# Latent attention scores by three passes over high and low parts, with the heads in two slots

## The chip, the cores and the metric

One core of one Trainium2 chip runs the whole program. The metric is the device time of one execution in microseconds (us); lower is better. All inputs and outputs are float32.

## What is computed

Two transformer blocks, one after the other, over 1024 tokens of width 1024. The change lies in the second block's latent attention (4 heads; each query and key has 128 plain and 64 rotated components; the rotated key is shared by the heads). Cut to what matters:

```python
q = (_rmsnorm(c_q, q_a_norm_w) @ w_uq).reshape(b, s, 4, 192)        # 128 plain + 64 rotated
kv = (_rmsnorm(c_kv, kv_a_norm_w) @ w_ukv).reshape(b, s, 4, 256)    # 128 key + 128 value
q_m = _rmsnorm(concatenate([q_nope, rope(q_rope)]), mla_q_norm_w)   # over 192
k_m = _rmsnorm(concatenate([k_nope, rope(k_rope)]), mla_k_norm_w)
s = einsum('bqhd,bkhd->bhqk', q_m, k_m) * 192 ** -0.5               # all 1024 keys, no mask
o = einsum('bhqk,bkhd->bqhd', softmax(s), v)
x = x + concatenate([o_mla, o_diff]) @ w_out
```

The second block also has a differential attention (ahead of the latent one) and an MLP (behind it). Nothing of the first block, of the differential attention or of the MLPs is changed.

## The kernel before

Activations lie transposed in SBUF: features in the 128 partitions, the 1024 tokens along the free dimension.
The order of the work is one list `S` of stages, written out by hand; each engine walks through all of `S` and issues its own part of each stage, so an engine that waits for one stage is not at the next. PSUM has two `big` tiles (128x1024), handed out by `take`, which waits until the reader of the tile's last use is done, two `tbank` tiles for transposes and two `obank` tiles for the outputs.

The latent part of `S`: the products `cq0`, `cq1`, `ckv`, `krope`, their norms, `uqr` (rotated queries of two heads at a time into `mqr[0]`, `mqr[1]`), then for each head h: `mh` h (24 matmuls at line 829: query, key, value, each drained by VectorE at line 1479), `v_t` (8 transposes of the values at line 870, copied out by ScalarE at line 1173), and for q and k each: `mn0` (ScalarE squares, line 1433; VectorE adds the rotated squares, line 1846), `mn1` (sum over the partitions by a product with ones, line 858), `mn2` (ScalarE takes the inverse root, Ln and Exp, lines 1185 and 1187; VectorE scales the plain and the rotated rows, lines 1853 and 1857). Heads 0 and 1 have `mh` and `v_t` ahead of the loop, heads 2 and 3 inside it.

The loop is `attend_pairs` over 32 units (4 heads x 4 steps x 2 query tiles of 128). In each iteration TensorE issues `sc` of the next unit (scores: 128 queries by 1024 keys, line 987; for each half of the keys one matmul over the 128 plain rows and one over the 64 rotated rows), then what `early` names, then half of the pair of the step before: `pv` part 0 (transposes of the probabilities, line 1010, and two of four groups of line 1028) or part 1 (the other two groups), then what `late` names. VectorE drains each score tile with its minimum (line 1705), later scales the probabilities (`nm`, lines 1725 and 1727); ScalarE takes the exponential (line 1221) and copies transposed probabilities out of PSUM (line 1173). `mn1` and `mn2` of the next head stand in iterations u + 2 and u + 4 of a head (u = 8h), ahead of `pv` part 0. `y2split` splits outputs for the next product and stands in the last head's odd iterations.

The queries and keys of all four heads have buffers of their own (`mqn`, `mkn`, `mqr`, `mkr`).

Of the kernel before, what the change touches and what calls it, by code (L numbers as in the profile page):

```python
# [15 lines left out]
F32 = mybir.dt.float32  # L16
# [97 lines left out]
def _emit(nc, ctx, known, a):  # L114
# [90 lines left out]
    sqr = [at(f"sqr{s}", G1 + 4 * K + 4 * K * s, [P, T]) for s in range(3)]  # L205
    cqf = [at(f"cqf{s}", G1 + 16 * K + 4 * K * s, [P, T]) for s in range(3)]
    krb = at("kr_b", G1 + 28 * K, [P, T])
    clh = at("cl_hi", G1 + 32 * K, [P, 3, T], F32R)
    cll = at("cl_lo", G1 + 44 * K, [P, 3, T], F32R)
    mqn = [at(f"mqn{h}", G2 + 4 * K * h, [P, T]) for h in range(4)]  # L210
    mkn = [at(f"mkn{h}", G2 + 16 * K + 4 * K * h, [P, T]) for h in range(4)]
    mqr = [at(f"mqr{p}", G2 + 32 * K + 4 * K * p, [P, T]) for p in range(2)]
    mkr = [at(f"mkr{p}", G2 + 40 * K + 4 * K * p, [P, T]) for p in range(2)]
    mvb = [at(f"mv{h}", G2 + 48 * K + 4 * K * h, [P, QT, P]) for h in range(4)]
    mpt = [at(f"mpt{s}", o, [P, HALF]) for s, o in enumerate((G2, G2 + 2 * K, G2 + 16 * K))]
    sqn = [at(f"sqn{s}", G1 + 16 * K + 4 * K * s, [P, T]) for s in range(2)]
    mrt = at("mrt", G1 + 24 * K, [P, T])
    mvf = at("mv_f", X0 + 28 * K, [P, T])
    sskv = at("ss_kv", G1 + 60 * K, [P, T])
    krz = at("kr_z", G1 + 56 * K, [P, T])  # L220
# [52 lines left out]
    s_hn = sig("head_normed")  # L273
    s_ptu = sig("pt_used")
# [310 lines left out]
    add("mh", 0)  # L585
    add("v_t", "mv0")
    for q in "qk":
        add("mn0", q, 0)
# [3 lines left out]
    add("mh", 1)  # L592
    add("v_t", "mv1")
    early, late = {}, {}
    for h in range(4):
        u = 8 * h
        if h == 3:
            late[u + 1] = [("y2split", 4), ("y2split", 5)]
            late[u + 3] = [("y2split", 6), ("y2split", 7)]
            late[u + 5] = [("y2split", 0), ("y2split", 1), ("y2split", 2)]  # L600
        else:
# [1577 lines left out]
```

## Time and profile before

| | |
|---|---|
| median of 3 runs | 3427.17 us (3426.89 to 3434.18) |
| the profiled execution | 3439.09 us |
| its span, first to last instruction | 3437.2 us |
| mean granted TensorE clock | 0.962 |
| TensorE matmul busy | 3188.8 us, 93% of the span |
| VectorE / ScalarE / GpSimd busy | 1214.4 / 1047.4 / 990.8 us |

How to read it: the span is the profiled execution less 1.9 us around it. Busy times of the engines overlap each other. "PEld" is the loading of TensorE's stationary operand, which can run beside a matmul. The end of a matmul is modelled, so the distance between starts is what to read for its cost. The granted clock is 1.0 at 2.4 GHz and 0.5 at 1.2 GHz.

### The profile page before, as it was taken

Reading aid. Unit: us, or ns where it says so; the run is one execution under the profiler, and the core shown is the slowest. Engines: PE = TensorE matmul, PEld = TensorE weight load, DVE = VectorE, ACT = ScalarE, POOL = GpSimd, SP = SyncE. Lnnn points to the kernel's source line nnn. Section 1 sums busy time; section 2 is a strip of 40 time slices with the busy share of each in tenths; the row PEclk is TensorE's granted clock in tenths of the full one; section 3 lists DMA queues with packets and bytes.
Section 4 is the critical chain, followed back from the end, with each engine's and each line's share of the span. In section 5 each row is a group of like instructions: output and inputs, shape, how many; then the busy total and the mean of one; then the engine's idle time right before and its main releaser. Section 6 shows DMA issues by size and latency. Waiting matters only on the chain. (4 is left out here: it accounts for less than half of the span.)

```text
span 3437.2 us, 36710 instructions
## 1 busy us (share of the span) xinstructions
PE 3188.8 (93%) x14286; PEld 2369.7 (69%) x14286; DVE 1214.4 (35%) x2184; ACT 1047.4 (30%) x1472; POOL 990.8 (29%) x416
## 2 busy tenths in 40 slices
PE   5989888888989999999999889887999999999998
PEld 3556555565778788888887556564446788888887
DVE  4347777766132111111113555734333211111111
ACT  3235544444442211111124344533333211111110
POOL 4322324121234343343347100031001332324241
PEclk8879998999999999999999999998999999999999
DMA  5311112111252111111111301010002111111112
GB/s 158 100 25 36 39 31 50 38 49 38 62 183 62 44 48 55 43 49 49 49 43 37 109 24 30 7 45 14 7 0 74 43 55 43 54 44 49 49 49 67
DMA packets 261614, 176.22 MB, mean 51 GB/s; under 512 B 20661, under 2 KB 248885, under 8 KB 260917
## 3 DMA queue, kind: packets, MB, share of 16 engines
q1 hardware_dynamic: 261496, 174.64, 17.5%
q8 instruction: 75, 1.23, 0.2%
q14 instruction: 43, 0.34, 0.0%
HBM read 142.60 MB, written 25.20 MB: 49 GB/s over the span
## 5 line engine op out<-in xcount | busy, mean ns | idle before, releaser
L829 PE MATMUL big<-g_hi,w_hi 128*128 128x512 f32 x3328 | 1072.8, 404 | 59.2 <-ACT gst_b L1247 21.1
L829 PE MATMUL big<-g_lo,w_hi 128*128 128x512 f32 x3328 | 1041.4, 394 | 0.0
L829 PE MATMUL big<-g_hi,w_lo 128*128 128x512 f32 x3328 | 1038.1, 393 | 0.0
L829 PEld LDWEIGHTS big<-g_hi,w_hi 128*128 128x128 f32 x3328 | 611.1, 191 | 257.1 <-issue 131.3
L829 PEld LDWEIGHTS big<-g_lo,w_hi 128*128 128x128 f32 x3328 | 633.2, 190 | 137.3 <-issue 0.7
L829 PEld LDWEIGHTS big<-g_hi,w_lo 128*128 128x128 f32 x3328 | 631.8, 190 | 137.5 <-issue 0.4
L1875 POOL TENSOR_TENSOR w_lo<-w_raw,w_hi 128x1024 fp32r<-128x1024 f32 x99 | 241.6, 2440 | 765.8 <-ACT w_hi L1149 765.8
L1953 POOL TENSOR_TENSOR w_lo<-w_raw,w_hi 128x1024 fp32r<-128x1024 f32 x76 | 181.9, 2394 | 64.2 <-ACT w_hi L1367 64.2
L1818 DVE TENSOR_TENSOR x_res<-big,x_res 128x1024 f32 x40 | 49.0, 1225 | 382.1 <-PE big L829 382.1
L1979 POOL TENSOR_TENSOR w_lo<-w_raw,w_hi 128x1024 fp32r<-128x1024 f32 x40 | 95.7, 2392 | 273.2 <-ACT w_hi L1395 273.2
L1173 ACT ACTIVATE pt<-tbank 128x512 f32<-128x512 f32 (+1 forms) x160 | 88.0, 554 | 221.8 <-PE tbank L1010 221.8
L1395 ACT ACTIVATE w_hi<-w_raw 128x1024 fp32r<-128x1024 f32 x40 | 42.4, 1060 | 327.4 <-PE big L829 327.4
L1964 POOL TENSOR_TENSOR g_lo<-t_act,g_hi 128x1024 f32 x32 | 76.7, 2397 | 217.1 <-ACT g_hi L1376 217.1
L1797 DVE TENSOR_TENSOR t_g<-big,r_rep 128x1024 f32<-128x1024 f32 x32 | 39.2, 1225 | 274.0 <-PE big L829 274.0
L1643 DVE TENSOR_SCALAR_CACHE_REDUCE tally_a<-idx_acc,edge 128x384 f32<-128x384 f32 (+2 forms) x147 | 126.6, 861 | 5.2
L1149 ACT ACTIVATE w_hi<-w_raw 128x1024 fp32r<-128x1024 f32 x99 | 103.7, 1047 | 74.0 <-PE big L829 57.0
L1376 ACT ACTIVATE g_hi<-t_act 128x1024 f32 x32 | 34.0, 1061 | 298.6 <-DVE t_act L1801 298.6
L1010 PE MATMUL tbank<-ident_sb,prob 128*128 128x128 f32 x576 | 97.5, 291 | 23.2 <-ACT prob L1215 21.0
L1915 POOL TENSOR_TENSOR gst_b<-gst_b,r_rep 128x1024 f32<-128x1024 f32 x16 | 38.3, 2391 | 273.6 <-ACT gst_b L1247 273.6
L1215 ACT ACTIVATE prob<-prob,rc 128x256 f32<-128x256 f32 (+7 forms) x128 | 92.1, 767 | 78.7 <-DVE rc L1718 78.7
L1010 PEld LDWEIGHTS tbank<-ident_sb,prob 128*128 128x128 f32 x576 | 71.5, 148 | 53.0 <-issue 19.2
L1790 DVE TENSOR_TENSOR t_act<-big,t_silu 128x1024 f32<-128x1024 f32 x22 | 26.9, 1225 | 214.3 <-PE big L829 214.3
(253 smaller groups left out, 3423.9 us busy)
## 6 DMA issues: line engine op xcount, KB each, us to landing
w_raw<-in_w_up SPq DMA_DIRECT2D x54, 512.0 KB, 4.0
w_raw<-in_w_in SPq DMA_DIRECT2D x51, 512.0 KB, 4.1
w_raw<-in_w_down SPq DMA_DIRECT2D x48, 512.0 KB, 4.1
w_raw<-in_w_gate SPq DMA_DIRECT2D x22, 512.0 KB, 3.8
rot<-rope_in SPq DMA_DIRECT2D x68, 128.0 KB, 2.3
g_spill<-gst_b SPq DMA_DIRECT2D x16, 512.0 KB, 3.0
x_res<-x_spill SPq DMA_DIRECT2D x2, 4096.0 KB, 14.6
w_raw<-in_w_out SPq DMA_DIRECT2D x16, 512.0 KB, 4.2
```

The lines of the kernel that those rows point to most:

```text
L829: ins = pe.matmul(out[0:m, HALF * h:HALF * h + HALF], w[slot][:, col:col + m], x[:, HALF * h:HALF * h + HALF], start=(n == 0 and q == 0), ...
L1010: ins = pe.transpose(tbank[tn[0] % 2][:, o:o + P], st["prob"][0][n % 2][:, ti, P * kt:P * kt + P], ident[:, :])
L1149: act.activation(w_hi[w % 2][:, :], w_raw[w % 2][:, :], ACT.Copy).then_inc(*s_whi.mark(w))
L1173: act.activation(dest, src, ACT.Copy).then_inc(*s_te.mark(*key))
L1215: act.activation(p, p, ACT.Copy, scale=rc[:, c:c + 1]).then_inc(*s_nrm.mark(s, lane))
L1395: act.activation(w_hi[sl][:, :], w_raw[sl][:, :], ACT.Copy).then_inc(s_whi.sem, 1)
L1643: dve.tensor_scalar(tally, z, edge[:, i:i + 1], 0.0, ALU.is_ge, ALU.add, accum_out=above[:, i:i + 1]).then_inc(*s_tk.mark("count", bit, i))
L1818: dve.tensor_tensor(xres[:, i * 2 + u, :], big[(p0 + u) % 2][:, :], xres[:, i * 2 + u, :], ALU.add).then_inc(s_rel.sem, 1)
L1875: pool.tensor_tensor(w_lo[s][:, :], w_raw[s][:, :], w_hi[s][:, :].bitcast(F32), ALU.subtract).then_inc(*s_wlo.mark(w))
L1953: pool.tensor_tensor(w_lo[sl][:, :], w_raw[sl][:, :], w_hi[sl][:, :].bitcast(F32), ALU.subtract).then_inc(s_wlo.sem, 1)
L1964: pool.tensor_tensor(g1l[:, i * 2 + u, :], tact[:, :], g1h[:, i * 2 + u, :].bitcast(F32), ALU.subtract).then_inc(s_mgl.sem, 1)
L1979: pool.tensor_tensor(w_lo[sl][:, :], w_raw[sl][:, :], w_hi[sl][:, :].bitcast(F32), ALU.subtract).then_inc(s_wlo.sem, 1)
```

## The change

The scores of a latent head are made of fp32r parts. For each head the plain queries and keys are split in high and low (`qnh`, `qnl`, `knh`, `knl`), three terms of 128 rows. The rotated part takes two terms: `rq` holds the high part of the rotated queries in one half of the partitions and the low part in the other, `rk` holds the high part of the rotated keys in both halves (one term of 128 rows, hi x hi and lo x hi together), and a term of 64 rows multiplies the high queries with the low keys `rkl`. The low half of `rq` is put in its place by a DMA from SP's queue. A new stage `mn3` makes the parts: ScalarE two copies for q and two for k, GpSimd two subtractions for q, VectorE two for k.

The buffers hold two heads at a time (`head_slot`), so head h + 2 waits for the last scores of head h; many smaller buffers move. One buffer `sqn` serves both squares, so `mn0` of k waits for `mn1` of q. In `S`, `mh` and `v_t` of head 1 move from ahead of the loop into it, like those of heads 2 and 3; these stages stand at u and u + 1 of the head before, `mn1`/`mn2` of q and k at u + 3 and u + 5, ahead of `pv` part 1, and `mn3` behind it. Ahead of the loop `mn0` of k now stands behind `mn2` of q, and `mn3` of both behind everything.

```diff
     add("mh", 0)
+    add("mn0", "q", 0)
     add("v_t", "mv0")
-    for q in "qk":
-        add("mn0", q, 0)
     for q in "qk":
         add("mn1", q, 0)
         add("mn2", q, 0)
-    add("mh", 1)
-    add("v_t", "mv1")
+        if q == "q":
+            add("mn0", "k", 0)
+    for q in "qk":
+        add("mn3", q, 0)
     early, late = {}, {}
-    for h in range(4):
+    for h in range(3):
         u = 8 * h
...
-            late[u] = [("mn0", "q", h + 1)]
-            early[u + 2] = [("mn1", "q", h + 1), ("mn2", "q", h + 1)]
-            late[u + 2] = [("mn0", "k", h + 1)]
-            early[u + 4] = [("mn1", "k", h + 1), ("mn2", "k", h + 1)]
-            if h < 2:
-                late[u + 5] = [("mh", h + 2)]
-                late[u + 6] = [("v_t", f"mv{h + 2}")]
+        late[u] = [("mh", h + 1)]
+        late[u + 1] = [("v_t", f"mv{h + 1}"), ("mn0", "q", h + 1)]
+        early[u + 3] = [("mn1", "q", h + 1), ("mn2", "q", h + 1)]
+        late[u + 3] = [("mn0", "k", h + 1), ("mn3", "q", h + 1)]
+        early[u + 5] = [("mn1", "k", h + 1), ("mn2", "k", h + 1)]
+        late[u + 5] = [("mn3", "k", h + 1)]
...
-                    maps=lambda lane: [[(mqn[c][:, :], mkn[c][:, :]), (half(mqr[c // 2], c % 2), half(mkr[c // 2], c % 2))]],
+                    maps=lambda lane: [[(qnh[c % 2][:, :], knh[c % 2][:, :]), (qnl[c % 2][:, :], knh[c % 2][:, :]),
+                                        (qnh[c % 2][:, :], knl[c % 2][:, :]), (rq[c % 2][:, :], rk[c % 2][:, :]),
+                                        (half(rq[c % 2], c % 2), half(rkl[c % 2], c % 2))]],
...
-                    "m": lambda: (s_hn.at("mq", c), s_hn.at("mk", c)),
+                    "m": lambda: (s_mlo.at(c), s_mlk.at("kr", c)),
...
+            elif stage == "mn3":
+                which, h = x
+                act.wait_ge(*s_hn.at(f"m{which}z", h))
+                hi, z = (qnh, qz) if which == "q" else (knh, kz)
+                act.activation(hi[h % 2][:, :], z[h % 2][:, :], ACT.Copy).then_inc(*s_mhi.mark(which, h))
+                act.wait_ge(*s_hn.at(f"m{which}", h))
+                if which == "q":
+                    r = slice(HD * (h % 2), HD * (h % 2) + HD)
+                    ins = act.activation(rq[h % 2][r, :], qrt[r, :], ACT.Copy)
+                else:
+                    ins = act.activation(rk[h % 2][:, :], rkz[h % 2][:, :], ACT.Copy)
+                ins.then_inc(*s_mhi.mark(which, "rope", h))
...
+                free = [s_big.at(*final_score(m_steps[h - 2][-1]))] if h >= 2 else []
+                scaled(("mh", h, "q"), qz[h % 2][:, :], big[pair[("mh", h, "q")]][:, :], r_rep[:, :], *free)
...
+            elif stage == "mn3" and x[0] == "k":
+                h = x[1]
+                dve.wait_ge(*s_mhi.at("k", h))
+                dve.tensor_tensor(knl[h % 2][:, :], kz[h % 2][:, :], knh[h % 2][:, :].bitcast(F32), ALU.subtract).then_inc(*s_mlk.mark("k", h))
+                dve.wait_ge(*s_mhi.at("k", "rope", h))
+                dve.tensor_tensor(rkl[h % 2][:, :], rkz[h % 2][:, :], rk[h % 2][:, :].bitcast(F32), ALU.subtract).then_inc(*s_mlk.mark("kr", h))
...
+            elif stage == "mn3" and x[0] == "q":
+                h = x[1]
+                r = slice(HD * (h % 2), HD * (h % 2) + HD)
+                pool.wait_ge(*s_mhi.at("q", h))
+                pool.tensor_tensor(qnl[h % 2][:, :], qz[h % 2][:, :], qnh[h % 2][:, :].bitcast(F32), ALU.subtract).then_inc(*s_mlq.mark("q", h))
+                pool.wait_ge(*s_mhi.at("q", "rope", h))
+                pool.wait_ge(*s_mlq.at("q", h))
+                pool.tensor_tensor(qrl[r, :], qrt[r, :], rq[h % 2][r, :].bitcast(F32), ALU.subtract).then_inc(*s_mlq.mark("rope", h))
+                pool.wait_ge(*s_mlq.at("rope", h))
...
+            elif stage == "mn3" and x[0] == "q":
+                h = x[1]
+                r, o = HD * (h % 2), HD * (1 - h % 2)
+                sp.wait_ge(*s_mlq.at("rope", h))
+                sp.dma_start(rq[h % 2][o:o + HD, :].bitcast(F32), qrl[r:r + HD, :].bitcast(F32)).then_inc(*s_mlo.mark(h, by=16))
```

## Rows read from the trace of the kernel before

**Rows 1.** The page, chain of work that ended last: shares of the span by line

```profile
PE big L829 24%; PE big L987 3%; PE obank L1028 2%; PE tbank L1010 1%; DMA x_res<-x_spill 0%; DMA out<-yst 0%; ACT mrt L1185 0%; ACT mpt L1173 0%; POOL w_lo L1875 0%; PE big L858 0%; PE tbank L870 0%; DVE yst L1864 0%; ACT dpt L1173 0%; DVE x_res L1768 0%; DVE mv_f L1479 0%
```

**Rows 2.** Windows: prologue, loop; PE, PEld, DVE, ACT, POOL busy us, clock, DMA

```profile
2297.00:2352.00 55.00, 33.92 (x105) 22.15 (x105) 26.54 (x18) 16.89 (x18) 21.34 (x9) 0.77 0.21 53
2352.00:2620.00 268.00, 251.79 (x858) 131.67 (x857) 109.86 (x174) 105.05 (x162) 4.80 (x2) 0.98 0.01 3
```

**Rows 3.** Timeline of TensorE in the loop: start us, us, line, operation, tile, count

```profile
2551.68 1.09 PE L1010 MATMUL tbank<-ident_sb,mprob 128*128 128x128 f32 x8
2553.12 1.10 PE L1028 MATMUL obank<-mpt,mv 128*128 128x256 f32 x4 [0.34 <-ACT mpt L1173]
...
2555.80 1.02 PE L987 MATMUL big<-mkn,mqn 128*128 128x512 f32 x2
...
2559.91 1.99 PE L1028 MATMUL obank<-mpt,mv 128*128 128x256 f32 x8
2561.75 1.02 PE L987 MATMUL big<-mkn,mqn 128*128 128x512 f32 x2
```

**Rows 4.** Chain in order of time: the last MLP's matmuls, start and length in us

```profile
2717.67 696.65 PE big L829 x3072
```

**Rows 5.** Timeline of TensorE's weight loads inside one score tile

```profile
2556.75 0.29 PEld L987 LDWEIGHTS big<-mkr,mqr 64*128 64x128 f32 x2 [0.76 <-issue]
```

**Rows 6.** Timeline of TensorE in the first block: line 829 beside other array shapes

```profile
608.72 0.63 PE L829 MATMUL big<-g_hi,w_lo 128*128 128x512 f32 x2
609.28 0.44 PE L1025 MATMUL obank<-pt,vb_b 128*64 128x128 f32 x4
...
610.28 0.73 PE L829 MATMUL big<-g_hi,w_hi 128*128 128x512 f32 x2
610.85 0.63 PE L829 MATMUL big<-g_lo,w_hi 128*128 128x512 f32 x2
```

**Rows 7.** Timeline of a key norm (TensorE, ScalarE, VectorE), and a second norm's TensorE

```profile
2387.62 1.98 PE L858 MATMUL big<-sqn,ones_sb 128*128 128x512 f32 x4
2389.45 1.04 PE L1010 MATMUL tbank<-ident_sb,mprob 128*128 128x128 f32 x8
2395.21 1.02 PE L987 MATMUL big<-mkn,mqn 128*128 128x512 f32 x2
...
2389.70 1.11 ACT L1185 ACTIVATE mrt<-big,eps_c 128x1024 f32<-128x1024 f32 x1 [5.31 <-issue]
...
2391.93 1.28 DVE L1853 SCALAR_TENSOR_TENSOR mkn<-mkn,gains,mrt 128x1024 f32<-128x1024 f32 x1 [2.88 <-ACT mrt L1187]
2394.75 0.75 DVE L1727 TENSOR_SCALAR mprob<-mprob,rc 128x1024 f32<-128x1024 f32 x1
...
2442.50 1.04 PE L1010 MATMUL tbank<-ident_sb,mprob 128*128 128x128 f32 x8
2449.94 1.02 PE L987 MATMUL big<-mkn,mqn 128*128 128x512 f32 x2
```

**Rows 8.** Timeline of head 2's products, and the group of all heads' value transposes

```profile
2400.97 0.82 PE L829 MATMUL big<-cl_hi,w_hi 128*128 128x512 f32 x2
2406.89 1.02 PE L987 MATMUL big<-mkn,mqn 128*128 128x512 f32 x2
...
L870 PE MATMUL tbank<-ident_sb,mv_f 128*128 128x128 f32 x32 | 6.4, 354 | 3.1 <-DVE mv_f L1479 2.6 <-ACT dpt L1173 0.3 <-ACT mpt L1173 0.3
```

**Rows 9.** Ahead of the loop: a DMA of the chain, then the timeline of all engines

```profile
2300.58 2.29 DMA rot<-kr_z
...
2329.60 5.70 PE L858 MATMUL big<-sqn,ones_sb 128*128 128x512 f32 x8 [4.49 <-DVE sqn L1846]
2341.53 2.51 POOL L1875 TENSOR_TENSOR w_lo<-w_raw,w_hi 128x1024 fp32r<-128x1024 f32 x1 [13.06 <-ACT w_hi L1149]
2341.75 3.37 DVE L1857 SCALAR_TENSOR_TENSOR mkr<-kr_b,gains,mrt 64x1024 f32<-64x1024 f32 x1
...
2352.33 1.06 PE L987 MATMUL big<-mkn,mqn 128*128 128x512 f32 x1
```

More of the change, by code:

```diff
@@ L213, in _emit @@
[L213 to L217, printed above, removed]
-    mvf = at("mv_f", X0 + 28 * K, [P, T])
-    sskv = at("ss_kv", G1 + 60 * K, [P, T])
-    krz = at("kr_z", G1 + 56 * K, [P, T])
+    sqrk, krb = at("sqr_k", G1 + 4 * K, [P, T]), at("kr_b", G1 + 8 * K, [P, T])
@@ new lines, in _emit, with head_slot @@
+    sqn = at("sqn", G1 + 48 * K, [P, T])
+    mrt, sskv = at("mrt", G1 + 52 * K, [P, T]), at("ss_kv", G1 + 52 * K, [P, T])
+    mvf = at("mv_f", X0 + 28 * K, [P, T])
+    def head_slot(name, offset, dt=F32R):
+        return [at(f"{name}{s}", G2 + (28 * s + offset) * K, [P, T], dt) for s in range(2)]
+    qnh, knh, rq, rk = head_slot("q_hi", 0), head_slot("k_hi", 8), head_slot("q_rope_hl", 16), head_slot("k_rope_hh", 20)
+    qnl, knl, rkl = head_slot("q_lo", 4), head_slot("k_lo", 12), head_slot("k_rope_lo", 24)
@@ L222, in _emit @@
+    qz, kz, rkz = head_slot("q_z", 4, F32), head_slot("k_z", 12, F32), head_slot("k_rope", 24, F32)
+    mvb = [at(f"mv{s}", G2 + 56 * K + 4 * K * s, [P, QT, P]) for s in range(2)]
     yst = [at(f"yst{s}", R0 + 4 * K * s, [P, QT, P]) for s in range(2)]
@@ L1113, in _ @@
             elif stage == "uqr":
-                terms = lambda pr: [(2 * P * k + P * pr, clh[:, k, :], cll[:, k, :], s_nl.at("q_a", k)) for k in range(2)]
+                terms = lambda pr: [(2 * P * k + P * pr, clh[k][:, :], cll[k][:, :], s_nl.at("q_a", k)) for k in range(2)]
                 for pr in range(2):
@@ L1126, in _ @@
                 pe.wait_ge(*s_mm.at("mn", which, h))
-                full_product(("mn", which, h), s_arel, [(ones[:, :], sqn[mnorms.index((which, h)) % 2][:, :])])
+                full_product(("mn", which, h), s_arel, [(ones[:, :], sqn[:, :])])
             elif stage == "yout":
@@ L1286, in _ @@
                 c = int(name[2])
[L1287 to L1288 removed]
+                dest = {"v": vab[c % 2], "d": dvb[c % 2], "m": mvb[c % 2]}[name[0]]
+                old = {"v": a_steps, "d": d_steps, "m": m_steps}.get(name[0], {}).get(c - 2)
                 for b in range(2):
@@ L1843, in _ @@
                 r = slice(HD * (h % 2), HD * (h % 2) + HD)
-                z, rope_sq = sqn[mnorms.index((which, h)) % 2], sqr[h // 2 if which == "q" else 2]
+                rows, rope_sq = (r, mrt) if which == "q" else (slice(0, HD), sqrk)
                 dve.wait_ge(*s_msq.at(which, h))
-                dve.tensor_tensor(z[r, :], z[r, :], rope_sq[r, :], ALU.add).then_inc(*s_mm.mark("mn", which, h))
+                dve.tensor_tensor(sqn[rows, :], sqn[rows, :], rope_sq[rows, :], ALU.add).then_inc(*s_mm.mark("mn", which, h))
@@ L1854, in _ @@
                 g = GAINS[f"m{which}_r"][0]
-                src = (mqr[h // 2] if which == "q" else krb)[r:r + HD, :]
-                dest = (mqr if which == "q" else mkr)[h // 2][r:r + HD, :]
-                dve.scalar_tensor_tensor(out=dest, in0=src, scalar=gains[r:r + HD, g:g + 1], in1=mrt[r:r + HD, :],
-                                         op0=ALU.mult, op1=ALU.mult).then_inc(*s_hn.mark("m" + which, h))
+                if which == "q":
+                    r = slice(HD * (h % 2), HD * (h % 2) + HD)
+                    dve.wait_ge(*(s_mlo.at(h - 1) if h else s_swap.at("uqr", 1)))
+                    if h == 0:
+                        dve.wait_ge(*s_cos.at("uqr", 1))
+                    src, dest, weight, root_ = mqr[h // 2][r, :], qrt[r, :], gains[r, g:g + 1], mrt[r, :]
+                else:
+                    src, dest, weight, root_ = krb[:, :], rkz[h % 2][:, :], gains[:, g:g + 1], mrt[:, :]
@@ new lines, in _ @@
+                dve.scalar_tensor_tensor(out=dest, in0=src, scalar=weight, in1=root_, op0=ALU.mult,
+                                         op1=ALU.mult).then_inc(*s_hn.mark(f"m{which}", h))
+            elif stage == "mn3" and x[0] == "k":
[4 more added lines that the diff above has]
+                dve.tensor_tensor(rkl[h % 2][:, :], rkz[h % 2][:, :], rk[h % 2][:, :].bitcast(F32), ALU.subtract).then_inc(*s_mlk.mark("kr", h))
```

67 lines of the change are left out of this document (32 added, 35 removed).

## The prediction

> **What bounds the kernel now.** I read first which chain ends last. Matmuls of line 829 carry most of it, and line 987, the scores, is the second name [rows 1]. So TensorE is the bound, and what matters is how it fares in the latent stage. The windows give that: in the loop TensorE is busy 251.8 of 268 us at a clock of 0.98, while VectorE and ScalarE have 110 and 105 us of work each; in the prologue TensorE is busy 34 of 55 us at 0.77, so there a chain of waits is the bound [rows 2]. Every instruction taken from TensorE in the loop shortens the time as long as VectorE and ScalarE keep up. In the prologue only the length of the chain counts.
>
> The timeline of TensorE then shows a steady pair of tiles [rows 3]: a score tile from 2555.80 to 2559.91 (4.11 us), part 1 of the products 1.84 us, another score tile, and part 0 from 2551.68 to 2555.80 (4.12 us, of which some is a wait for ScalarE's first copy out of PSUM, 2553.12). Together 14.18 us, 16 times. The scores are 32 x 4.11 = 131.5 us.
>
> **The score tile.** Before: 4 calls, 8 MATMUL instructions. After: 10 fp32r matmuls of 512 columns. The price of one is best read where nothing else happens: 3072 of them in 696.65 us, 0.227 us each, every one with its own weight load [rows 4]. Ten are 2.27 us. But the old tile isn't a multiple of one number either. The load of the 64-row term's weights starts only after TensorE's load side was idle for 0.76 us [rows 5]: it is not brought forward under the running matmul, as it is between products of equal height. The sum of squares, four equal instructions from 2387.62 to 2389.45, takes 1.83 us, some 0.43 us each with a small start [rows 7]; eight would be 3.41 us, and the tile takes 4.11. The 0.70 us go to the changes of height, four to a tile with the one at its end. Does an fp32r matmul pay for them too? The nearest rows are those of line 829 beside products that use another part of the array: the start behind two of them comes after 0.56 us instead of 0.455 (608.72 to 609.28), and the first two back on full height take 0.57 us (610.28 to 610.85) [rows 6]. That is 0.1 + 0.1 us for one change, the same as 0.70 / 4 within what a row can tell. The new tile has four terms of full height and one of 64 rows, twice: again four changes. So I take 2.27 + 0.70 = 2.97 us. It saves 1.14 us, and 32 tiles save 36.5 us. The bounds are 2.27 us (changes are free for fp32r, saving 58.9 us) and 10 x (0.227 + 0.20) = 4.27 us (each change of weights costs what a change of height does, losing 5.1 us).
>
> The Trainium skill, page "TensorE: Matmul & The Clock Gate", Part 3, "What overlaps and what doesn't", says that weight loads overlap with running matmuls only when the row group differs. By it the full-height terms would not overlap and the 64-row term would; the tile would come near the upper bound. The trace says the opposite: equal heights overlap [rows 4] and a change of height waits [rows 5]. I follow the trace and keep the rule as the slower rival.
>
> **Head 1's products and values move into the loop.** They lay in the prologue beside the key norm of head 0. In the loop nothing covers them, since TensorE is the bound. The like of head 2 takes 2400.97 to 2406.89, 5.92 us, and the transposes of a head 6.4 / 4 = 1.6 us [rows 8]. Together +7.5 us. Their split of the next weights (one ScalarE copy, one GpSimd subtraction) and the load on SP move along; GpSimd has 4.8 us of work in the loop, so that is hidden.
>
> **The norms in the loop.** There are six (q and k of heads 1 to 3). Before, ScalarE did Ln and Exp ahead of the first copy for part 0, so part 0 took 2389.45 to 2395.21, 5.76 us instead of 4.12: +1.64 [rows 7]. In three of the six TensorE went on slower after that wait (2442.50 to 2449.94, 7.44 us: +3.3). Sum 3 x 1.64 + 3 x 3.3 = 14.8 us. After, the norm stands ahead of part 1, whose copies are long made, so this wait goes. What is late next is the scaling `nm`: on VectorE it stands behind the two scalings of `mn2`, and the transposes of the next part 0 wait for it. Count from the end of the score tile ahead of the norm. Ln starts 2.08 us after the product does (2387.62, 2389.70), the first scaling 4.31 us (2391.93), and the probabilities are ready at 2394.75 + 0.75, 7.9 us after it [rows 7]. TensorE does meanwhile the product (1.83), part 1 (1.84) and a score tile (2.97) and is at the transposes after 6.64 us. It waits 1.2 us; behind the query norm ScalarE has also the square of k and two copies of `mn3` to make, about 0.3 us more. Six such waits are 3 x 1.2 + 3 x 1.5 = 8.1 us; for a slower clock behind some of them I add 2.2 us, since they are shorter than the 3 us before. Together 10.3 us, a change of -4.5. Bounds: 0 (everything hidden) and 20 us (all six as slow as 2442.50).
>
> What `mn3` adds for each head: ScalarE four copies, near 1 us each, VectorE two subtractions of about 1.2 us, GpSimd two of 2.5 us and a DMA, all of it with owners that are idle over half of the loop [rows 2]. The queries' low rotated rows are placed about 15.5 us after the query norm's score tile (ready copies at 8.8, GpSimd's two steps, 2.3 us for the DMA as in [rows 9]); the next head's first tile comes four tiles later, past 25 us. The keys are ready 10.7 us after their norm's tile and wanted at 12. That margin of 1.3 us is the thinnest; in the range I give it 0 to 2 us for each of three heads. Behind `mn3` on VectorE's queue stands the drain of the tile that has just been done, but the two PSUM tiles in hand are free by then. `y2split` now meets shorter tiles: in iteration 29 its three copies hold ScalarE's first copy for part 0 about 0.6 us: +0.6.
>
> **The prologue.** Before, the first score starts at 2352.33 [rows 9], after head 1's products. After, the chain is: first square at 2319.4 instead of 2325.6; product with ones behind the value transposes at 2325.1; Ln 3.9 us later, at the low clock seen there (2329.60, 8 instructions in 5.70 us [rows 9]); Exp, two scalings; then k's squares, sum (2335.0), Ln and Exp until 2341.0, its scaling until 2342.3. Before, the two norms overlapped in part; now they follow one another. Then `mn3`: GpSimd starts the low queries at 2342.3, and VectorE's scaling of the rotated key meets it. In the trace the like took 3.37 us instead of 1.27, until GpSimd's subtraction was over [rows 9]. GpSimd and VectorE so take turns: 2344.7, 2345.9, 2348.3; the DMA lands at about 2351.3. VectorE's last subtraction ends at 2350.8. First score 2351.3, 1.0 us sooner than before, and 0.8 us are lost again to a longer stretch at the low clock, as nothing runs on TensorE for 12 us before it. Net -0.2. Bounds 2349.9 (no collisions) to 2355.5 (the first sum of squares also waits for GpSimd's three steps in a row).
>
> The Trainium skill, page "SBUF — State Buffer", "SBUF: two separate sides", says that VectorE and GpSimd hold a shared port pair for a whole instruction, the other one blocked. The trace agrees (3.37 us). In a sum without it the DMA lands 1.4 us sooner.
>
> **Sum.** -36.5 + 7.5 - 4.5 + 0.6 - 0.2 = -33.1 us. On the profiled execution (3439.09 us, span 3437.2) that gives 3406.0. It was 11.9 us above the median of 3427.17; I take the same difference off the median: 3394.
>
> **The rivals.**
>
> 1. Changes of height cost fp32r nothing. Tile 2.27 us, saving 58.9; the waits at the norms grow by 0.7 us each (+4.2), and `y2split` takes 1.3 more. Change -50: 3377. For it: none of the rows of line 829 is next to an fp32r product of 64 rows. Against it: rows 6. Chance 0.12.
> 2. The helpers bound more than I count: the key's margin is gone in three heads (+6), norm waits at their upper bound (+9.7), start at 2355.5 (+4.2). Change -13: 3414. For it: VectorE's queue is in strict order and now holds four more long steps in a head. Against it: each engine is under half busy. Chance 0.13.
> 3. Slower: each weight load is exposed in the score tile, where every matmul has other weights than the one before. Tile 4.27 us: +5.1 instead of -36.5, with the other terms +3.4: +8.5, 3436. It decides from 0.40 us for a matmul, where the tile saves no more than the 3.4 us that the other terms cost. Against it: rows 4 have 3072 loads, all hidden. Chance 0.04.
> 4. The change doesn't do what it says, as when the scores still ran as two instructions for each term: ten terms at 0.43 x 2 would be 8.6 us a tile, far slower (+140). The diff gives all ten operands the type that line 829 has; chance 0.01.
>
> The forecast has 0.70. The range of 8 in 10 leaves out rivals 3 and 4 and the outer halves of 1 and 2: 3377 to 3410. About 0.2% (7 us) is what a measurement of this kernel tells from no change. Rivals 3 and 4 are slower or nearly; of rival 2 a small part is within 7 us. Faster 0.93, same 0.02, slower 0.05.
>
> **What would show it.** Line 987 has 320 fp32r matmuls, and a steady score tile takes 2.97 us from start to start, with gaps in the load row at the 64-row term; a pair takes 11.9 us. The first score starts near 2351, the last product ends some 33 us sooner, near 2587. At the norms part 0's transposes start 1 to 2 us late, released by VectorE's line 1727. The prediction is wrong if tiles are at 2.3 us, if the first tile of heads 1 to 3 waits for the placed DMA or the low keys, or if the clock in the loop is well below 0.98.

## The result, and the profile after

The changed kernel takes 3398.35 us (median of 4 runs, 3394.96 to 3406.64) against 3427.28 (3426.89 to 3434.18): ratio 0.9914, 95% interval 0.9892 to 0.9937. Forecast was 3394, range 3377 to 3410, faster. Its profiled execution took 3395.90 us, span 3394.1, against 3439.09 and 3437.2: 43.1 us less, of which only part belongs to the change, as the measure below shows.

The windows of the changed kernel, prologue and loop of the latent stage (window, length, then busy us of TensorE, its weight loads, VectorE, ScalarE, GpSimd, then granted clock, DMA share, GB/s); they answer to [rows 2]:

```profile
2292.90:2344.10 51.20, 25.57 (x73) 15.40 (x71) 26.58 (x17) 19.57 (x20) 25.49 (x10) 0.75 0.21 51
2344.10:2580.80 236.70, 221.99 (x953) 153.56 (x954) 127.73 (x183) 119.52 (x177) 24.62 (x9) 0.98 0.03 9
```

The prologue is 51 us instead of 55, the loop 237 instead of 268, and TensorE is still busy for 94% of the loop. To compare kernels I use one measure all through, *the stage*: from the start of VectorE's drain of the rotated keys (`kr_z`) to the start of ScalarE's last `g_hi`, both in the chain of waits. Before it is 2297.49 to 2620.92, 323.4 us; after, 2292.86 to 2581.27, 288.4 us. So 35.0 of the 43.1 us are in the stage; 4.6 lie ahead of it and some 3.5 behind it, in code that is the same (the load of `x_res` took 14.21 and 12.99 us). The medians differ by 28.9 us, and the interval of the ratio allows 22 to 37.

TensorE's timeline in the loop, a steady pair; it answers to [rows 3]. Where single matmuls are listed, a record's length contains its filling, and what counts is start to start:

```profile
2531.77 1.09 PE L1013 MATMUL tbank<-ident_sb,mprob 128*128 128x128 f32 x8
2533.20 1.10 PE L1031 MATMUL obank<-mpt,mv 128*128 128x256 f32 x4 [0.34 <-ACT mpt L1176]
...
2541.18 0.39 PE L990 MATMUL big<-k_lo,q_hi 128*128 128x512 f32 x1
2541.41 0.40 PE L990 MATMUL big<-k_rope_hh,q_rope_hl 128*128 128x512 f32 x1
2541.73 0.49 PE L990 MATMUL big<-k_rope_lo,q_rope_hl 64*128 64x512 f32 x1
2542.16 0.50 PE L990 MATMUL big<-k_hi,q_hi 128*128 128x512 f32 x1
2542.49 0.39 PE L990 MATMUL big<-k_hi,q_lo 128*128 128x512 f32 x1
...
2543.71 1.09 PE L1013 MATMUL tbank<-ident_sb,mprob 128*128 128x128 f32 x8
```

The pair takes 11.94 us instead of 14.18. Matmuls of equal height follow each other after 0.23 us, the one of 64 rows starts 0.32 after the one ahead of it, the next of full height 0.43 after that, and the one behind it 0.33: 0.09, 0.20 and 0.10 more than 0.23, some 0.39 us for the two changes. The weight loads in the tile before show the same two gaps:

```profile
2536.35 0.19 PEld L990 LDWEIGHTS big<-k_rope_hh,q_rope_hl 128*128 128x128 f32 x1
2536.91 0.18 PEld L990 LDWEIGHTS big<-k_rope_lo,q_rope_hl 64*128 64x128 f32 x1 [0.37 <-issue]
2537.34 0.19 PEld L990 LDWEIGHTS big<-k_hi,q_hi 128*128 128x128 f32 x1 [0.24 <-issue]
```

The list of TensorE's waits in the loop (us in total, times, longest):

```profile
PE big L990 <- DMA q_rope_hl<-q_rope_lo: 12.2, 1, 12.2
PE tbank L1013 <- DVE mprob L1746: 7.3, 6, 1.4
PE obank L1031 <- ACT mpt L1176: 6.8, 17, 1.0
```

The DMA holds only the very first score. At each of the six norms the transposes wait 1.1 to 1.4 us for the normalization (`nm`, the scaling of the probabilities), and the waits of 2.04 us for ScalarE's copy, six in the kernel before, are gone. The timeline of TensorE and VectorE at the first query norm shows the order on VectorE's queue that makes this wait:

```profile
2381.06 1.06 PE L1013 MATMUL tbank<-ident_sb,mprob 128*128 128x128 f32 x8 [1.38 <-DVE mprob L1746]
...
2377.37 1.28 DVE L1871 SCALAR_TENSOR_TENSOR q_z<-q_z,gains,mrt 128x1024 f32<-128x1024 f32 x1 [2.88 <-ACT mrt L1190]
2378.69 1.29 DVE L1882 SCALAR_TENSOR_TENSOR q_rope<-mqr,gains,mrt 64x1024 f32<-64x1024 f32 x1
2380.01 0.16 DVE L1744 RECIPROCAL rc<-sm 128x1 f32<-128x1 f32 x1
2380.21 0.75 DVE L1746 TENSOR_SCALAR mprob<-mprob,rc 128x1024 f32<-128x1024 f32 x1
```

Both multiplications of the norm go ahead of the normalization that TensorE wants.

### The profile page after: what moved, and what is told of

Same layout as the page of the kernel before. It is cut to its first block and busy times, and to the rows that moved or that the text cites. A ratio compares the mean times of both kernels' runs of the same rounds, so it can differ in the third digit from the quotient of the medians.

```text
span 3394.1 us, 36893 instructions
## 1 busy us (share of the span) xinstructions
PE 3144.6 (93%) x14350; PEld 2380.6 (70%) x14350; DVE 1231.7 (36%) x2192; ACT 1065.0 (31%) x1490; POOL 1014.8 (30%) x424
```

## The experiments

Eleven kernels ran, on four chips; each ratio is to the kernel before on the same chip (`e1` to `e4` 3431.27 us, `e5` to `e8` 3437.1, `e9` and `e10` 3434.15, `e11` 3438.21). Stages are those of the profiled executions, one of each kernel, and I don't read a difference of under 2 us between two of them. What repeated executions of one kernel would give for the stage isn't known: the low clock alone costs its loop between 1.0 and 14.2 us, by kernel. The intervals of the changed kernel, `e2`, `e4` and `e5` overlap, so what sets these apart is shown by the stage and its rows, not by the whole kernel.

### The change of height

`e1`: the fifth term takes all 128 rows, which adds the product of the low rotated queries with the low keys and leaves nothing out.

```diff
-                                        (half(rq[c % 2], c % 2), half(rkl[c % 2], c % 2))]],
+                                        (rq[c % 2][:, :], rkl[c % 2][:, :])]],
```

> The fifth score term runs over all 128 rows of rq and rkl instead of 64 (it adds low x low of the rotated part, so nothing is left out). My theory: each change of the array's height costs about 0.16 us, four to a tile; the tile falls from 2.91 to 2.3 us, 32 tiles give 19.6 us, of which some 4 come back, since TensorE reaches each of the six norm waits 0.6 us sooner: about -15 us against the changed kernel. Rival: the 0.1 to 0.2 us belong to the start of each half of the keys or to the number of different weights, not to the height: the tile stays at 2.9 us and the time within 3 us.

Measured: 3381.67 us, ratio 0.9856 (0.9828 to 0.9884); the stage 273.1 us, 15.3 below the changed kernel. Its tile in the chain of waits, the start of part 0 in two steady pairs that follow each other, and its list of waits:

```profile
2535.72 2.30 PE big L990 x10
...
2521.12 1.04 PE L1013 MATMUL tbank<-ident_sb,mprob 128*128 128x128 f32 x8
2531.50 1.04 PE L1013 MATMUL tbank<-ident_sb,mprob 128*128 128x128 f32 x8
...
PE tbank L1013 <- DVE mprob L1746: 10.8, 6, 2.0
```

In the changed kernel the same chain has 2.88 to 2.93 us for a tile, 0.61 more; but it cuts off what the last change of a tile costs the products behind it (part 1 takes 1.54 us here and 1.64 there). The pair has all of it: 10.38 us instead of 11.94. So eight changes of height cost 1.56 us, 0.195 each. Between its matmuls this tile has the 0.23 us of the first rival's 2.27, with 128 rows instead of 64: more rows, less time. Of 16 x 1.56 = 25.0 us the waits take back 3.5 (normalization), 1.7 (copies, 8.5 instead of 6.8) and 1.0 (the next weights' turn, 1.5 instead of 0.5), the first score comes 1.0 us later, and the low clock costs the loop 7.5 us instead of 5.7: 16.0 are left, where 15.3 are measured.

`e2`: the second half of each tile runs its terms backwards, so that the two products of 64 rows meet and a tile has two changes instead of four.

```diff
-for q, (qa, ka) in enumerate(terms):
+for q, (qa, ka) in enumerate(terms[::-1] if kind == "m" and n0 else terms):
```

> The second half of the keys takes its five terms in reverse order, so the two 64-row terms stand together: two changes of height to a tile instead of four, same matmuls. My theory: tile 2.91 - 2 x 0.16 = 2.6 us, 10 us from 32 tiles less 2 us given back at the norm waits: about -8 us. Rival (cost sits at the start of a half or with the 64-row matmul itself): tile unchanged at 2.9 us.

Measured: 3388.03 us, ratio 0.9869 (0.9836 to 0.9903), the stage 278.7 us, -9.7. TensorE's timeline in it, the middle of a tile and the start of part 0 in two pairs that follow each other:

```profile
2500.02 0.40 PE L990 MATMUL big<-k_rope_hh,q_rope_hl 128*128 128x512 f32 x1
2500.34 0.73 PE L990 MATMUL big<-k_rope_lo,q_rope_hl 64*128 64x512 f32 x2
2501.00 0.50 PE L990 MATMUL big<-k_rope_hh,q_rope_hl 128*128 128x512 f32 x1
...
2529.46 1.04 PE L1013 MATMUL tbank<-ident_sb,mprob 128*128 128x128 f32 x8
2540.68 1.04 PE L1013 MATMUL tbank<-ident_sb,mprob 128*128 128x128 f32 x8
```

Two products of 64 rows back to back take 0.66 us from start to start, where each alone took 0.43 and passed 0.10 on to the next. The pair takes 11.22 us, 0.72 less than in the changed kernel with four changes fewer, 0.18 for each. The products are the same, only their order in the sum differs, so the cost is not that of a product of 64 rows. In this order the two products of 64 rows use the same weights one after the other; `e1`, where the height never changes, has 0.23 us also where the weights do change, so the gap goes with the height and not with new weights.

### What the layout and the norm's place are worth without the new tile

`e3`: the scores as two float32 terms over the high parts; the low parts are made and not used, so the scores lack them.

```diff
-                    maps=lambda lane: [[(qnh[c % 2][:, :], knh[c % 2][:, :]), (qnl[c % 2][:, :], knh[c % 2][:, :]),
...
+                    maps=lambda lane: [[(qnh[c % 2][:, :].bitcast(F32), knh[c % 2][:, :].bitcast(F32)),
+                                        (half(rq[c % 2], c % 2).bitcast(F32), half(rk[c % 2], c % 2).bitcast(F32))]],
```

> The new layout and order, all of mn3 too, but the scores as two plain float32 terms over the high parts (the low parts of queries and keys are left out of the scores). It measures what the change costs without its gain in the tile. My theory: tile back at 4.1 us, all else as after; at 4.1 us TensorE reaches the transposes 7.8 us after the tile ahead of a norm, about when the probabilities are ready, so the norm waits are near 0. Against the kernel before: +7.5 (head 1's products) - 14.8 (norm waits) - 2.6 (start) = about -10 us. Rival: mn3's eight steps a head on the helpers cost time of their own, or the new places of the norms do not pay: 0 to +5 us against before.

Measured: 3430.82 us, ratio 1.0001 (0.9985 to 1.0017); the stage 320.0 us, 31.6 above the changed kernel and 3.4 below the one before (10 were expected). So the change without its tile is worth nothing that the whole kernel shows. The waits for the normalization were near 0 (the long tile covers them), as expected; where did their gain go? Its windows, the start of the loop and the rest:

```profile
2344.50:2366.00 21.50, 21.43 (x29) 8.24 (x30) 3.29 (x6) 3.42 (x5) 2.34 (x1) 0.50 0.01 4
2366.00:2613.00 247.00, 240.92 (x862) 128.37 (x861) 123.50 (x177) 116.32 (x172) 22.22 (x8) 1.00 0.03 8
```

TensorE had been idle for 12.2 us ahead of its first score; then it ran 21.5 us at the lower of its two levels (0.50), the first tiles and head 1's products among them, at a loss of 10.7 us. In the kernel before, head 1's products stand there and the loop starts with 0.9 us lost.

`e4`: the changed kernel with head 1's products and transposes ahead of the loop again.

```diff
-    for q in "qk":
-        add("mn3", q, 0)
+    add("mn3", "q", 0)
+    add("mh", 1)
+    add("mn3", "k", 0)
+    add("v_t", "mv1")
...
-        late[u] = [("mh", h + 1)]
-        late[u + 1] = [("v_t", f"mv{h + 1}"), ("mn0", "q", h + 1)]
+        late[u] = [("mh", h + 1)] if h else []
+        late[u + 1] = ([("v_t", f"mv{h + 1}")] if h else []) + [("mn0", "q", h + 1)]
```

> mh and v_t of head 1 are back ahead of the loop, between mn3 of q and mn3 of k of head 0, where TensorE waits 12 us for the low rotated queries. My theory: the 7.5 us that they cost in the loop go, the first score starts within 1 us of where it does now, since the DMA is last: about -7 us. Rival: the drains of the products on VectorE stand ahead of the low keys and the products run at the low clock, so the first score starts 3 us or more later and the gain is under 4 us.

Measured: 3394.95 us, ratio 0.9891 (0.9862 to 0.9920), the stage 281.0 us, -7.4. The chain of waits ahead of the first score:

```profile
2337.91 4.09 PE big L834 x18
2341.99 4.07 issue
2346.07 2.91 PE big L834 x6
...
2350.28 1.97 PE tbank L875 x8
...
2352.59 7.61 PE big L992 x21
```

The first score comes 54.6 us after the stage's start instead of 51.2, 3.4 us later, as the rival had it: the last six products and the transposes run at half clock here (2.91 us where the loop has 1.62). Yet the sum is the theory's. The loop saves its 7.3 us, and it loses 2.7 us to the low clock instead of 5.7 (sums as in the section on the terms). Of these 3.0 us, 1.2 are gained at the loop's start, where part of the slow stretch after the long wait now lies under the products and transposes. The other 1.8 are gained behind the norms, which the edit doesn't touch: that the sum came out as expected is in part luck.

`e8`: both edits, `e3` and `e4` together, so that tile and start are those of the kernel before and only layout and norms differ.

> The kernel with the scores as two float32 terms over the high parts (the low parts are made but not used, so the scores lack their low parts), in the new layout and order, with head 1's products and transposes ahead of the loop as in the kernel before. The tile then costs what it did (4.02 to 4.11 us) and so does the order at the start, and what is left of the difference to the kernel before is the norm alone: the wait of TensorE for it was 14.8 us in the stage before. The float32 scores in the order of the changed kernel took 3.4 us off the stage, not the 7 to 10 expected. Theory 1 (the low clock at the start ate it: 21.3 us of the loop at 1.2 GHz against 6 in the kernel before, because head 1's products no longer stand in that stretch): the stage now takes about 323.4 - 14.3 = 309 us, 11 us below that kernel's 320.0. Theory 2 (the norm waits were worth less than their sum because TensorE catches up behind them): about 317 us.

Measured: 3433.3 us, ratio 0.9976 (0.9948 to 1.0004). The stage is 2289.88 to 2596.62, 306.7 us: 16.7 below the kernel before, 13.3 below `e3`. From the timeline of its start:

```profile
2343.48 2.04 PE L991 MATMUL big<-k_hi,q_hi 128*128 128x512 f32 x2 [0.34 <-issue]
2345.45 1.16 PE L991 MATMUL big<-k_rope_hh,q_rope_hl 64*128 64x512 f32 x2
```

The second pair is at full clock already. Theory 1 holds in these rows (309 expected). The 16.7 us are made up, within a microsecond, of the norms' waits that are gone (10.2), less low clock in the loop (1.0 us lost instead of 5.9) and an earlier first score (53.6 us into the stage instead of 54.8); in `e3` 10.7 us of low clock and head 1's place in the loop ate this gain. It rests on one execution of each kernel, and that of `e8` took 3413.15 us, 20 less than its median; the whole kernel's interval (0.9948 to 1.0004) doesn't tell it from no change.

### The waits for the normalization

`e5`: the norm's root (ScalarE) and its multiplications (VectorE) stand behind the normalization.

```diff
-        early[u + 3] = [("mn1", "q", h + 1), ("mn2", "q", h + 1)]
-        late[u + 3] = [("mn0", "k", h + 1), ("mn3", "q", h + 1)]
-        early[u + 5] = [("mn1", "k", h + 1), ("mn2", "k", h + 1)]
-        late[u + 5] = [("mn3", "k", h + 1)]
+        early[u + 3] = [("mn1", "q", h + 1)]
+        late[u + 3] = [("mn2", "q", h + 1), ("mn0", "k", h + 1), ("mn3", "q", h + 1)]
+        early[u + 5] = [("mn1", "k", h + 1)]
+        late[u + 5] = [("mn2", "k", h + 1), ("mn3", "k", h + 1)]
```

> The changed kernel with one thing moved: VectorE's two multiplications of a head's norm (its own part and the rotated part, by weight and root) stand behind the normalization of the tile beside them on VectorE's queue, no longer ahead of it. In the changed kernel TensorE waits 7.3 us in six places for that normalization (the longest 1.4), because 2.6 us of multiplications go first while the exponentials have already ended (at 2378.4 and 2395.2 in the first two places, where the normalization ends at 2380.95 and 2397.4 and TensorE stood ready at about 2379.7 and 2396.4). Theory of the document's step 3 (the wait is the order on VectorE's queue): the six waits go, tbank<-VectorE falls from 7.3 us to under 1, and with the one low-clock stretch behind them the stage falls from 288.4 to about 280, 7 to 8 us faster than the changed kernel. Rival (the wait is only moved): the parts of queries and keys come 1 to 2 us later, the key's last part then at about 2401.4 instead of 2400.1 for the second head, and TensorE waits for it or for the drain of the tile that stands behind the multiplications, ahead of the scores or transposes of the next head; then no more than 2 us are gained and new waits of 1 to 2 us stand at the first tiles of heads 1 to 3.

Measured: 3397.67 us, ratio 0.9883 (0.9852 to 0.9914). The stage is 2283.46 to 2569.07, 285.6 us, only 2.8 below the changed kernel (0.5 us less of these waits, and 3.8 us lost to the low clock instead of 5.7). (What was moved is both steps, ScalarE's root too, which the text on record doesn't name.) TensorE's list of waits has no line for the normalization any more, but this one, and the timeline shows it at the first query norm:

```profile
PE obank L1031 <- ACT mpt L1176: 13.6, 17, 1.6
...
2372.68 1.10 PE L1031 MATMUL obank<-mpt,mv 128*128 128x256 f32 x4 [1.63 <-ACT mpt L1176]
...
2369.54 1.06 ACT L1444 ACTIVATE q_hi<-q_z 128x1024 fp32r<-128x1024 f32 x1 [0.40 <-DVE q_z L1871]
2370.86 1.05 ACT L1448 ACTIVATE q_rope_hl<-q_rope 64x1024 fp32r<-64x1024 f32 x1 [0.26 <-DVE q_rope L1882]
2371.94 1.09 ACT L1176 ACTIVATE mpt<-tbank 128x512 f32<-128x512 f32 x2
```

The cause of the wait was the one named: behind the root and the multiplications. Moving them takes 7.3 us of waits off VectorE's queue and puts 6.8 on ScalarE's: the roundings into high parts, which now wait for VectorE, stand ahead of the copies of the transposes. The rival's places (the next head's first scores) were wrong, its size (no more than 2 us) was nearly right.

`e9`: the splits (`mn3`) one tile later, behind those copies.

```diff
+        late[u + 4] = [("mn3", "q", h + 1)]
         early[u + 5] = [("mn1", "k", h + 1)]
-        late[u + 5] = [("mn2", "k", h + 1), ("mn3", "k", h + 1)]
+        late[u + 5] = [("mn2", "k", h + 1)]
+        late[u + 6] = [("mn3", "k", h + 1)]
```

> The kernel with the norm's root and multiplications behind the normalization, with one more thing moved: the splits of the multiplied queries and keys into high and low parts (ScalarE's two roundings, the subtractions, the DMA to the other half) stand one tile later, behind the products of the next tile's first part and so behind the two copies of its transposes. In the kernel with the norm behind the normalization, all six waits for the normalization were gone, but TensorE waited 13.6 us for ScalarE's copies of the transposes where the changed kernel had 6.8, because at the six norms the copies stood behind two roundings (2369.54 to 2371.9) that themselves waited for VectorE; the stage took 285.6 us, only 2.8 below the changed kernel. Theory (the wait went over to ScalarE's queue, and nothing else holds the rest): with the roundings behind the copies the waits for copies fall back to 6 to 8 us and those for the normalization stay near 0, and the stage takes about 278 to 280 us. Rival (the drains of VectorE and ScalarE as a whole have become the pace, in whatever order): the wait shows again at the tile in which the splits now stand, and the stage stays at 284 to 287.

Measured: 3415.11 us, ratio 0.9947 (0.9931 to 0.9964); the stage is 2305.14 to 2605.58, 300.4 us: 12 us worse than the changed kernel. Both theory and rival missed. From its waits, and TensorE's and VectorE's timelines at the start of the second head:

```profile
PE big L992 <- issue: 12.2, 3, 4.1
PE obank L1033 <- ACT mpt L1178: 6.5, 16, 1.0
...
2414.71 0.77 PE L992 MATMUL big<-k_hi,q_hi 128*128 128x512 f32 x1 [4.08 <-issue]
...
2413.39 1.22 DVE L1891 TENSOR_TENSOR k_rope_lo<-k_rope,k_rope_hh 128x1024 fp32r<-128x1024 f32 x1
```

The copies no longer wait (6.5 us in 16 places, most of them the usual 0.34), but the key's last low part now ends at 2414.6, 4.1 us after TensorE wanted it. The like happens in each of three heads, and the tiles behind run at half clock for some microseconds (the loop loses 14.2 us to the low clock instead of 5.7). This is the margin that the prediction called the thinnest, crossed from the other side.

### Together

`e7`: full height and head 1 ahead. `e6`: the same with the norm behind the normalization. `e10`: `e6` with both splits later. `e11`: `e6` with only the query's split later (`late[u + 4]`). None leaves anything out.

> The changed kernel with two of the edits measured alone: the fifth term of each tile over all 128 rows (no change of array height; the low-by-low product of the rotated part comes in beside it), and head 1's products and its values' transposes ahead of the loop, between the norm's last step of head 0's query and that of its key. Nothing of the computation is left out. Alone they took 15.3 and 7.4 us off the stage. If they are independent, the stage takes 288.4 - 15.3 - 7.4 = 265.7 us. Rival: the first edit has left the stage nearer to the drains of VectorE and ScalarE (waits for the normalization rose from 7.3 to 10.8 us in it alone), and the two overlap at the start, where the clock is low in either, so that 3 to 5 us of the sum are lost (269 to 271).

> All three: the fifth term over all 128 rows, head 1's products ahead of the loop, and the multiplications of the norm behind the normalization. Nothing of the computation is left out. If the edits are independent, the stage takes 265.7 us less the normalization's waits, which were 10.8 us with the full height: about 256 us, and the kernel about 3365 us. Rival: with a tile of 2.30 us TensorE comes to the next head's first scores sooner, at a time when the key's low parts, now 1.3 to 2 us later, are not there; then it is no faster than the kernel with the two edits alone (266 us for the stage), and the waits stand at the first tiles of heads 1 to 3.

> The same order of the norm (root and multiplications behind the normalization, splits one tile later) together with the fifth term over all 128 rows and head 1's products ahead of the loop. Nothing of the computation is left out. The kernel with these without the later splits took 262.65 us for the stage and waited 20.5 us for copies of the transposes. Theory: the twelve or so us above the 8.1 that the waits for copies cost with the two edits alone go, and the stage takes about 250 to 252 us. Rival: with a tile of 2.30 us a pair is shorter than what ScalarE and VectorE do beside it at the norms, and half or more of the waits stay: 256 to 262.

> The kernel with the full height, head 1's products ahead of the loop and the norm behind the normalization (its stage took 262.65 us, with 20.5 us of waits for ScalarE's copies of the transposes), and of the splits only the query's one tile later. With the key's one tile later too, TensorE waited 4 to 5.4 us at the first scores of each of heads 1 to 3 for the key's low parts (ready at 2414.6 in the first of them) and then ran at the low clock; the query's split has two tiles more until its head begins. Theory (each split costs the copies behind it about 2 us where it stands, and only the key's has a due time that is near): the three waits at the query's norms (the first of them 2.58 us) fall to about 0.7, those at the key's stay (2.3 us), no tile of heads 1 to 3 waits for a part, and the stage takes 262.65 - 3 x 1.9 = about 257 us. Rival (one slow stretch less is given back in the next): VectorE's addition for the key's sum of squares and GpSimd's subtraction of the query then collide elsewhere, and the stage stays within 2 us of 262.65. Nothing of the computation is left out.

| kernel | median us | ratio to before (95%) | stage us | waits for normalization, for copies us |
|---|---|---|---|---|
| changed | 3398.35 | 0.9914 (0.9892 to 0.9937) | 288.4 | 7.3, 6.8 |
| `e7` | 3375.74 | 0.9821 (0.9793 to 0.9850) | 263.7 | 11.0, 8.1 |
| `e6` | 3374.65 | 0.9816 (0.9784 to 0.9847) | 262.7 | 0.2, 20.5 |
| `e10` | 3381.45 | 0.9838 (0.9810 to 0.9866) | 272.0 | 0.2, 8.2 |
| `e11` | 3374.04 | 0.9821 (0.9790 to 0.9852) | 259.2 | 0.2, 17.2 |

Full height and head 1's place add up (24.7 us; 22.7 expected). The norm's place brings 1.1 us on top of them, not the 10 of the theory; 10.8 us of waits for the normalization became 12.4 for the copies, so the rival had the size and not the place (no tile of heads 1 to 3 waits for the keys). `e10` waits 5.1 to 5.4 us for the keys in each of three heads, as `e9` does, and missed its theory (250 to 252) and its rival (256 to 262) with 272.0. In `e11` the query's waits fell to 0.34 us, further than the 0.7 of the theory, but the key's grew from 2.33 to 3.45, 3.20 and 3.45, the first, at 2390.48, with the low clock behind it:

```profile
2375.25 1.10 PE L1034 MATMUL obank<-mpt,mv 128*128 128x256 f32 x4 [0.34 <-ACT mpt L1179]
2390.48 2.05 PE L1034 MATMUL obank<-mpt,mv 128*128 128x256 f32 x4 [3.45 <-ACT mpt L1179]
```

The stage is 3.4 us shorter, between the theory (5.7) and the rival (under 2), and the waits for copies 3.3. `e6`, `e7` and `e11` beat both the kernel before and the changed one by clear margins; which of them is best the whole kernel doesn't tell. `e7` is the simplest.

## Why the prediction was right, and where its terms were off

Here each term is set beside what the profile of the changed kernel has. The losses to the low clock are sums of (1 - granted clock) x length over windows of some 10 us.

| term | predicted us | measured us | from |
|---|---|---|---|
| 32 score tiles | -36.5 | -35.8 | 16 pairs, 11.94 instead of 14.18 |
| head 1's products and values in the loop | +7.5 | +7.3 | 2352.32 to 2358.70, and 2361.72 to 2362.57 |
| the norms, with the clock behind them | -4.5 | -4.4 | see below |
| `y2split` | +0.6 | +1.0 | one wait of 1.04 |
| first score | -1.0 | -3.6 | 51.2 instead of 54.8 us into the stage |
| low clock at the loop's start | +0.8 | +1.4 | 2.3 us lost instead of 0.9 |
| sum | -33.1 | -34.1 | the stage itself: -35.0 |

0.9 us remain unassigned. The forecast took 33.1 us off the median; the medians differ by 28.9, and runs of one kernel differ by more than the 4 us between. How the medians' difference divides into the stage and the rest isn't known, since only the profiled executions have a stage.

**The tile.** Predicted 2.97 us from 2.27 plus 0.70, 1.14 less than before. The pair gives 1.12 less for each tile. From start to start the two tiles of a steady pair take 3.09 and 3.18 us, more than predicted, and the products behind them 1.64 and 4.03 instead of 1.84 and 4.12: the sum is right, its split is not, so part of the closeness is luck. `e1` and `e2` show that the reason was right: without changes of height the pair is 1.56 us shorter, 0.195 for each change, taken as 0.175. The old tile's 0.70 / 4 and the 0.2 us of rows 6 lie on either side of it; rows 6 show a change to 64 columns of the array and not to 64 rows, so their closeness proves little. The first rival (changes free) is refuted by `e1` and `e2`, the third (each load exposed) by the 0.23 us between equal heights. The page "TensorE: Matmul & The Clock Gate" in the Trainium skill, Part 3, "What overlaps and what doesn't", says that loads overlap with running matmuls only where the row group differs. The traces here don't agree: at equal heights the matmuls follow each other after 0.23 us, each with its own load, and the load side idles where the height changes (0.37 and 0.24 us). No two neighbouring products here lie in separate rows, so for that case they say nothing.

**The norms.** Before, six waits of 2.04 us where 0.34 is the rule, 10.2 us, and about 5.0 us lost to the clock behind three: 15.2, predicted 14.8. After, 7.3 us of waits (predicted 8.1) and some 3.5 us lost behind two (predicted 2.2): 10.8 against 10.3. The step "what is late next is `nm` behind `mn2`" is shown by the rows above, and `e5` shows it to be the cause, since the wait goes when the order does (with ScalarE's root moved too). What the prediction didn't see is the next in line, ScalarE's copies behind `mn3`'s roundings.

**Head 1.** Right in sum by two misses: the products cost 6.4 us, not 5.92 (0.55 us of waiting for the next weights' turn, 2357.24), and the transposes 0.87, not 1.6, because two of the four heads' transposes in the L870 group of [rows 8] ran at the low clock (records of 1.97 us, at 2323.14 and 2350.57, where the record here has 1.09 and the next start comes after 0.85). `e4` took off 7.4.

**`y2split`.** The size was nearly right, the route was wrong. Not ScalarE's first copy is held: VectorE does three subtractions, the last tile's drain stands behind them, and its exponentials hold the copies of part 1. From the chain of waits and the timeline of the last tiles:

```profile
2566.46 1.93 DVE g_lo L1772 x2
...
2568.74 1.22 DVE g_lo L1772
2569.95 1.15 DVE mprob L1724 x2
...
2572.91 1.99 PE L1031 MATMUL obank<-mpt,mv 128*128 128x256 f32 x8 [1.04 <-ACT mpt L1176]
```

**The prologue.** This is the mis-sized term: 1.0 us predicted, 3.6 measured. The two products with ones show why, with what held the second:

```profile
2320.17 1.98 PE L861 MATMUL big<-sqn,ones_sb 128*128 128x512 f32 x4
2328.15 3.72 PE L861 MATMUL big<-sqn,ones_sb 128*128 128x512 f32 x4 [6.00 <-DVE sqn L1865]
2344.07 0.79 PE L990 MATMUL big<-k_hi,q_hi 128*128 128x512 f32 x1 [12.20 <-DMA q_rope_hl<-q_rope_lo]
```

I had given the first the low clock of rows 9 (3.9 us until the root starts), and it ran at full clock and took 2.1; only the second was slow. The first stands right behind the value transposes, which ran at full clock too (1.09 us), while in [rows 9] the product stood behind a wait of 4.49 us; that this is the reason isn't shown. GpSimd so starts on the low queries 42.3 us into the stage instead of 44.8, and the rest of the chain has the predicted length. The collisions between GpSimd and VectorE happened as described: VectorE's step on the rotated key took 3.37 us and the subtraction behind it 3.36 instead of 1.22. The DMA took 3.03 us. The prediction names 2.3 for it, from a DMA of half its size in [rows 9] (128 KB, not 256), but its own times leave 3.0 us from GpSimd's end to the landing (2348.3 to 2351.3):

```profile
2335.39 3.37 DVE L1882 SCALAR_TENSOR_TENSOR k_rope<-kr_b,gains,mrt 128x1024 f32<-128x1024 f32 x1
2338.69 3.36 DVE L1887 TENSOR_TENSOR k_lo<-k_z,k_hi 128x1024 fp32r<-128x1024 f32 x1
...
2340.99 3.03 DMA q_rope_hl<-q_rope_lo
```

**The second rival** (the helpers bound more) had none of its three parts: the key's margin held in every head, the norm waits stayed near their estimate, the start came sooner. In the kernels with a shorter tile it begins to come true: the waits for the normalization rise to 10.8 us in `e1`, those for the copies to 20.5 in `e6`.

## What to carry over

Count a matmul's price by its neighbours: where one operand fills 64 rows and the next 128, each change cost TensorE 0.2 us here, nearly a matmul's time (0.23), and filling the other half with a product that isn't needed was cheaper than leaving it empty. When a step in a strict queue holds the bounding engine, ask for each helper what is moved behind what: here the wait went from VectorE to ScalarE, and then to the next head's first scores. And work that is moved out of a stretch in which the bounding engine idles can be paid twice, for its own time and for the low clock that it used to absorb (`e3` against `e8`).

## What the runs showed of the hardware

- A product of 128 x 512 in fp32r over all rows costs 0.23 us also when it computes something unneeded; a change between 128 and 64 rows costs 0.18 to 0.195 us by the steady pair (`e1`, `e2`), and two products of 64 rows in a row pay for going there and back once (`e2`).
- After 12.2 us without work TensorE ran at half clock for 21.3 us with float32 scores (`e3`), but for 4.4 to 8.0 us with fp32r scores (4.7 in the changed kernel, 4.4 in `e1`, 8.0 in `e2`), after the same wait. In both it was busy throughout (21.43 us of 21.50; 9.90 of the changed kernel's first 9.90). Each is one execution, and no run tells why the one comes back so much later.
- Beside `mn3`'s subtractions on GpSimd a VectorE step of 1.22 to 1.28 us took 3.36 or 3.37 us, and two in a row did so. Not every meeting is like that: at 2318.91 VectorE's addition of squares took its 1.21 us, and GpSimd's step beside it 3.36 us instead of 2.37.
